# The normed input, turned by fp32 products of x with a diagonal matrix instead of scaled and transposed

## What is computed

```
def rms_norm(x, g):
    y = x * lax.rsqrt(jnp.mean(x * x, axis=-1, keepdims=True) + NORM_EPS)
    return y * g
# first block:   x = x + rms_norm(stage(rms_norm(x, pre_g)), post_g)
# second block:  x = x + gate * stage(rms_norm(x, g) * (1 + scale) + shift)
```

## Times and profile before

| | us |
|---|---|
| median of 3 runs | 1985.28 (1984.87 to 1985.38) |
| the profiled execution | 1984.69 |
| its span | 1982.9 |
| PE busy | 1876.9 |
| DVE busy | 1426.4 |
| ACT busy | 1174.9 |
| mean granted clock of PE | 0.985 of full |

### The profile page before, as it was taken

The page is one execution under the profiler, slowest core; times in us unless marked ns, Lnnn a source line. Parts: engine busy times, 40 slices in busy tenths (PEclk is TensorE's granted clock), DMA queues, the critical chain, the costliest instruction groups (busy, mean ns, idle before and its releaser), DMA issues.

```text
span 1982.9 us, 36008 instructions
## 1 busy us (share of the span) xinstructions
PE 1876.9 (95%) x14638; PEld 1724.7 (87%) x14638; DVE 1426.4 (72%) x2196; ACT 1174.9 (59%) x2092; POOL 12.8 (1%) x25
## 2 busy tenths in 40 slices
PE   8898999898989998999999999999999998999998
PEld 7887999887779997999889967799989998879998
DVE  5677877754677777877778776877787777576555
ACT  6544666664666557656676675655666566575332
POOL 0000000020000000000000000000000000000000
PEclk9999999999999999999999999999999999999999
DMA  8303666354057654888444402687858872324551
GB/s 328 115 4 150 228 230 223 136 182 160 19 193 256 241 201 176 329 287 287 148 148 160 170 1 75 248 310 275 292 213 308 279 278 96 123 96 161 190 191 54
DMA packets 96357, 374.98 MB, mean 189 GB/s; under 512 B 5824, under 2 KB 6464, under 8 KB 95424
## 3 DMA queue, kind: packets, MB, share of 16 engines
q1 hardware_dynamic: 95552, 372.15, 52.1%
q10 hardware_dynamic: 640, 0.52, 0.1%
HBM read 371.08 MB, written 1.05 MB: 188 GB/s over the span
## 4 chain that ended last, share of the span: by engine, by line
PE 79%; DVE 12%; ACT 6%; issue 3%; ACTq 0%; DMA 0%; DVEq 0%; SPq 0%
PE psum L1104 35%; PE psum L1120 17%; PE psum L782 9%; PE psum L875 4%; DVE buf L676 2%; PE psum L1735 1%; DVE htok L3019 1%; PE psum L3128 1%; PE psum L740 1%; PE psum L3587 1%; DVE x_res L535 1%; PE psum L2621 1%; DVE htok L534 1%; DVE buf L1025 1%; ACT buf L670 1%
## 5 line engine op out<-in xcount | busy, mean ns | idle before, releaser
L1104 PEld LDWEIGHTS psum<-buf,buf 128*128 128x128 f32 x6048 | 740.9, 192 | 14.6 <-DVE buf L996 6.0
L1104 PE MATMUL psum<-buf,buf 128*128 128x256 f32 x6048 | 744.6, 283 | 4.8 <-DVE buf L996 4.8
L1120 PE MATMUL psum<-buf,buf 128*128 128x512 f32 x1584 | 382.5, 391 | 3.0 <-DVE buf L1170 3.0
L1120 PEld LDWEIGHTS psum<-buf,buf 128*128 128x128 f32 x1584 | 289.6, 188 | 59.6 <-DVE buf L1170 4.4
L996 DVE TENSOR_TENSOR buf<-ring,buf 128x1024 fp32r<-128x1024 f32 x264 | 311.0, 1220 | 8.8 <-DVE modT L1052 7.5
L990 ACT ACTIVATE buf<-ring 128x1024 fp32r<-128x1024 f32 x264 | 263.2, 1046 | 0.0
L782 PE MATMUL psum<-buf,buf 128*128 128x256 f32 x1944 | 246.9, 287 | 11.6 <-DVE buf L676 11.1
L782 PEld LDWEIGHTS psum<-buf,buf 128*128 128x128 f32 x1944 | 238.6, 193 | 17.8 <-DVE buf L676 16.3
L1012 DVE TENSOR_TENSOR buf<-ring,buf 128x1024 fp32r<-128x1024 f32 x132 | 161.6, 1224 | 83.9 <-ACT buf L1007 83.9
L1007 ACT ACTIVATE buf<-ring 128x1024 fp32r<-128x1024 f32 x132 | 139.4, 1056 | 85.0 <-PE psum L1120 82.0
L1025 DVE TENSOR_TENSOR buf<-buf,crow 128x1024 f32<-128x1024 f32 x144 | 171.8, 1218 | 0.0
(11 more groups left out here) (431 smaller groups left out, 2025.8 us busy)
## 6 DMA issues: line engine op xcount, KB each, us to landing
ring<-in_w_ffn SPq DMA_DIRECT2D x88, 1536.0 KB, 6.9
buf<-in_w_mod SPq DMA_DIRECT2D x144, 512.0 KB, 4.8
ring<-in_w_conv SPq DMA_DIRECT2D x44, 1536.0 KB, 6.5
ring<-in_w_ssd_in SPq DMA_DIRECT2D x16, 1536.0 KB, 6.4
ring<-in_w_ns_in SPq DMA_DIRECT2D x7, 1536.0 KB, 6.5
ring<-in_w_hy_in SPq DMA_DIRECT2D x6, 1536.0 KB, 14.8
ring<-in_w_ssd_out SPq DMA_DIRECT2D x5, 1536.0 KB, 6.8
ring<-in_w_cmp SPq DMA_DIRECT2D x4, 1024.0 KB, 5.3
```

Source lines behind the costliest of these rows:

```text
L1104: ins = E.matmul(b[:, g * T:(g + 1) * T], w[:, wa, g, k, :], h[:, ha, k, :], start=k + n_ == 0, stop=k == KC - 1 and n_ == 2)
L1120: ins = E.matmul(acc[:, t, g * 512:(g + 1) * 512], hr[z][:, ha, t * P:(t + 1) * P], wd[j][:, wa, g * 512:(g + 1) * 512], start=j == 0 and ...
```

## The change

The square goes to `hT`'s memory instead of `htok`'s. DVE no longer scales x: it multiplies the identity by the column of inverse roots, which gives a 128x128 diagonal matrix, kept in the first 128 columns of each tile of `htok`. PE then takes each block of x itself as the stationary operand and the diagonal as the moving one, in a plain fp32 matmul in place of a transpose; the product is the block transposed and scaled. Tile 1 has one wait instead of two.

```diff
+            unread = hT_[:, :].rearrange("p (t d) -> p t d", t=NT)
+
+            def diagonal(t):
+                return htok[:, t, 0:P]
...
-                    squared.append(al(A.activation(htok[:, t, ds], x[:, t, ds], ACT.Square, accum_out=sums).then_inc(act.sem, 1)))
+                    squared.append(al(A.activation(unread[:, t, ds], x[:, t, ds], ACT.Square, accum_out=sums).then_inc(act.sem, 1)))
...
                     vl(V.reciprocal(sx[:, t:t + 1], sx[:, t:t + 1]).then_inc(dve.sem, 1))
-                    for at, ds in THIRDS:
-                        if at == t:
-                            scaled.append(dve.count(V.tensor_scalar(htok[:, t, ds], x[:, t, ds], sx[:, t:t + 1], None,
-                                                                    ALU.mult).then_inc(dve.sem, 1)))
+                    scaled.append(dve.count(V.tensor_scalar(diagonal(t), ident, sx[:, t:t + 1], None,
+                                                            ALU.mult).then_inc(dve.sem, 1)))
...
-            def turn(ks, t, half):
+            def turn(ks, t):
 
                 @block.tensor
                 def _(_e):
-                    E.wait_ge(*scaled[t + half])
+                    E.wait_ge(*scaled[t])
                     for k in ks:
-                        ins = E.transpose(turned(k)[:, t * P:(t + 1) * P], htok[:, t, k * P:(k + 1) * P], ident)
+                        ins = E.matmul(turned(k)[:, t * P:(t + 1) * P], x[:, t, k * P:(k + 1) * P], diagonal(t), start=True, stop=True)
                         if t:
                             moved[k] = pe.count(ins.then_inc(pe.sem, 1))
...
-            turn(range(KC), 0, 0)
+            turn(range(KC), 0)
             for k in range(4):
-                turn((k,), 1, 0)
-                turn((k + 4,), 1, 1)
+                turn((k,), 1)
+                turn((k + 4,), 1)
```

## The result

The changed kernel takes 1988.17 us (median of 20 runs, 1984.53 to 1993.71) and the kernel before 1983.56 (20 runs, 1977.53 to 1986.44). The ratio is 1.0029, 95% interval 1.0021 to 1.0037: slower by 0.29%, 5.8 us (the medians alone differ by 4.6). The forecast was +6.2. The forecast time, 1991.5, is 3.3 above the measured 1988.2; 1.7 of that is the reference, since the three runs of the kernel before on which the forecast stood had a median of 1985.28.

A forecast was written before the change was run, and what follows sets the result against it. PE, busy 95% of the span, was taken as the bound. Norms 1 to 5 +6.3, 6 to 9 +0.3, 10 -0.4: +6.2 on 1984.69 gives 1990.9; with 0.59 for the median, 1991.5 us, range 1987.0 to 1994.5.

The forecast's parts named there:

- Two instructions per product: In the turning, each fp32 product is two PE instructions: 32 instead of 16 per norm, 0.112 us each, 0.213 at low clock.
- The price of four transposes: In the turning, a product costing four transposes, 0.44 us where the rows give 0.22; the kernel would end near 2040.
- the third rival: Whole kernel: a product at the price of four transposes, or a loss that nothing shows; over 1996 us, chance 0.03.
- The scaling at 0.27: On DVE at L572, scaling the 128x128 identity by the column of roots takes 0.27 us.
- Norms 6 to 9, +0.07 each: Sixth to ninth of ten edited norms, at full clock: first block at 970.89 instead of 970.83 in norm 6; +0.3 for four.
- Norm 10, -0.4: Last of ten edited norms: the clock holds, and 48 matmuls end at 1795.86 instead of 1796.31.
- Norms 2 to 5, +1.8, +1.7, +1.5, +1.0: Second to fifth edited norms: doubled turning at the low clock delays the end of the next stage's first 48 matmuls, in us.
- Norm 1, +0.3: First edited norm: DVE's split begins at 13.2 instead of 12.94, after a later first block; +0.3 us.
- The first rival: Norms 2 and 3: products without pause raise the clock earlier, costing 0.2 and 0.3; total +3.2, 1988.5 us, chance 0.22.
- The second rival: In the turning, each product's second instruction hides, under about 0.06 us at full clock; total -4.4, 1980.9 us, chance 0.03.
- My sign of being wrong: Forecast wrong if norm 6 differs by more than 0.3 us or the low-clock norms end within 0.5 of today's.
- the long stretches (+8.6) with a fall in norm 10: Norms 4 and 5 stay at low clock as long as norm 2, total +8.6; with norm 10's clock falling, +9.2.

The follow-up runs named there:

- The halves of the change: The change in norms 1 to 5 alone, others as before: 1.0035 to the kernel before; in norms 6 to 10 alone: 1.0003.
- one instruction per block: Changed kernel with blocks turned by transposes of x against the identity, still waiting for the diagonal, root scaling left out: 0.9994 to the kernel before.
- the repeated one: The changed kernel measured and profiled again, nothing altered: 1.0025 to the kernel before.
- the doubled tile 0: Changed kernel with each product of tile 0 issued twice into the same place, 48 instructions per norm: 1.0124 to the kernel before.
- the squares alone: Kernel before with only the squares sent to hT, scaling and transposes as before: 1.0007 to the kernel before.
- the kernel before, filled: Old scaling and transposes, with PE's pause ahead of norms 2 to 5 filled by unread identity products: 1.0002 to the kernel before.

## Why the prediction was right, point by point

- **Two instructions per product, as many as L649 shows.** Right: 320 MATMULs, one every 0.112 at the full clock and 0.213 at the low one, as forecast. Only the first gap of each turning was wider, 0.21 in norm 6 and 0.38 in norm 2, which I had at nothing; so 32 took 3.84 us in norm 6 and not 3.7.
- **The price of four transposes.** The Trainium skill ("TensorE: Matmul & The Clock Gate", Terms) has the transpose mode four times faster for FP32. The trace doesn't agree: two instructions against one, 0.112 us apart and, for the transposes before, 0.109, both in tile 0 of norm 6 behind the first gap; a factor of two per block. That also rules out the third rival's first half.
- **The scaling at 0.27.** It took 0.287.
- **Norms 6 to 9, +0.07 each.** +0.15: the right size, off by the two terms above. The halves of the change agree, 1.0003 for norms 6 to 10.
- **Norm 10, -0.4, because the clock holds.** It held; -0.15. The kernel with norms 6 to 10 alone shows -0.4, and in the others PE's pause behind the gate products was 0.23 longer than I took it. The reason that I gave, the shorter pause, isn't shown: with one instruction per block PE started as early and the clock fell, and with norms 1 to 5 alone norm 10 has the old way and the clock held.
- **Norms 2 to 5, +1.8, +1.7, +1.5, +1.0.** Measured +0.8, +1.7, +1.4, +1.9. The way to the first block is right (tile 1 waits for PE, first block 4.7 behind the turning's start, 4.55 forecast). Mis-sized is how long the clock stays low from there. In norm 2 I let the blocks follow 0.85 apart until 200.7; the clock was back at 197.6, and ACT took all eight in 3.29 us. In norm 5 I had the clock rise 3.4 behind the turning's start; the norm had moved by 1.9, and it lasted to 777.9, 5.3 behind. These are the stretches that I had named as able to move, but the sum came out, +5.8 for +6.0, by luck: -1.0 and +0.9 nearly cancelled.
- **Norm 1, +0.3.** Between -0.2 and +0.7 in two profiles, and it varies by 2 us between kernels in which it is the same, so no run here settles it.
- **The first rival, an earlier clock.** In norm 2 of the first profile the clock was back earlier than I had it, at a cost of 0.8 where the rival has 0.2. In the repeated one it came as the rival has it, back after 3.4 us, and norm 2 is 0.2 above the profile before; in norm 3 it stayed low for 5.6 us or more behind the turning's start in both. My sign of being wrong, low norms within 0.5 of today's, is thus met by one norm of one profile.
- **The second rival, a hidden instruction.** Excluded by the doubled tile 0: 16 instructions more took 1.78 us, 0.111 each, and the rival needs under 0.06.
- **What I had missed.** I compared with norms 2 and 3 of one profile, in which the low clock reached into the 48 matmuls (15.92 and 16.18). Others have 15.15 and 15.55. Against those the change costs 1.0 to 1.5 in norm 2 and 2.0 to 2.3 in norm 3, over the two profiles of the changed kernel. The sum was right partly because the changed norm 2 was cheaper by about as much as the reference was dear. And the upper end of the range has a slip: the long stretches (+8.6) with a fall in norm 10 (+0.5 for -0.4) make +9.5 and not +9.2.

## What to carry to other kernels

A transformation that moves work from an idle engine to PE should be priced at the clock that PE has in that place. Here, behind a pause of 4 to 5 us, it was the low one, and the same second instructions that cost 0.15 us net per norm at the full clock cost 1.0 to 2.3 there. Look for the cover of both forms: at either clock the 16 transposes fitted under the other engines' chain to within 0.2 us in norms 2 to 4, and twice as many instructions did not at the low one. If the pause can't be removed, products that nobody reads can hold the clock, but they are worth something only once PE is what the stage ends on: they took the loss from the changed kernel and gave the kernel before nothing.

## What the runs showed of the hardware

- The clock can stay low for longer under a shorter PE job. With one instruction per block it was 0.50 from 191.8 to 202.0 in norm 2, 10.2 us, and for as long in norms 3 and 4; with two, from 190.8 to 197.6 in the first profile and from 192.4 to 195.8 in the second. The number of instructions alone isn't the reason: the squares alone, with 16 transposes too, had 6.8 us in norms 2 to 4. PE starts 0.5 us earlier and waits in other places there; which of it keeps the clock low was not tried.
- Plain fp32 products of the identity with itself, nearly without pause, kept the clock at 1.00 through a stretch in which it otherwise fell, in 15 of the 16 norms where they were tried (norms 2 to 5 of four kernels); the exception is norm 5 of the kernel before, filled.
- The executions of the kernel before range over 0.45% (1977.53 to 1986.44). Traces of different kernels differ in where the stretches at 0.50 lie inside the attention stages; whether that is what spreads one kernel's time was not tried.
